# A transformer layer's feed-forward part: weight sums made once by adding DMA transfers, weights loaded in pieces of 512 columns, and the first two output projections run one after the other

## The chip, the cores and the metric

The kernel runs on one core of a Trainium2 chip. The metric is the device time in microseconds (us) of one launch. Five engines work side by side, each on its own list of instructions: PE (TensorE, matrix products; its weight loads are listed apart as PEld), DVE (VectorE), ACT (ScalarE), POOL (GpSimd) and SP (SyncE, which here only issues DMA transfers). They wait for each other through semaphores.

## The reference

For 2048 tokens of width 1024 in float32:

```
h    = rmsnorm(x);  q, k, v of two attention groups = h @ w_in
mix  = concat(differential attention, stick-breaking attention)
x1   = x + mix @ w_out                                # 1024 x 1024
h2   = rmsnorm(x1) * g_ffn
x2   = x1 + (silu(h2 @ w_gate) * (h2 @ w_up)) @ w_down  # width 2816
out  = rmsnorm(x2) * g_final
```

## The kernel before

The program has three stages: projections (0 to 595 us, the function `phase_project`, with a barrier of all engines at its end), attention (595 to about 1485 us), and the output projection with the feed-forward part (the rest, `ffn_programs`). The third stage is the one that is rebuilt.

**Precision.** PE multiplies float32 values as three products: each operand is split into a high part, which ACT writes (`split_hi`, tile `whi` for weights), and a low part, which DVE writes as operand minus high part (`split_lo`, tile `wlo`, line 1665). Only hi*hi, hi*lo and lo*hi are computed. A piece of weights of 128 x 512 is a *unit*. There are seven pairs of `whi` and `wlo` (RING = 7), so a unit can be split as soon as PE has multiplied the one seven before it.

**Blocks and phases.** Tokens go in 4 blocks b of 512. For each block:

- `project(b)`: x1 of block b, 16 units of 12 matmuls each (lines 2108 and 2118). The mixed heads are first turned by PE (`mix_turns`, line 2132, 32 transposes a block) out of the tile `natural`; ACT and DVE split the result (`thi`, `tlo`, lines 1698 and 1929).
- a norm of x1 (`square`, `variance`, POOL's `power`, `scale_in`), 32 transposes of the result on PE (`h2_turns`, line 2154; for block 0 line 2142), copies back (`act_plain`, `dve_plain`), and the seven *operands* of the next phase, split into hi and lo (`prepare_hi`, `prepare_lo`). Four of the operands (s1 to s4) are sums of quarters of h2, made by POOL (`low_sums`, `high_sums`, lines 1611 to 1622).
- `gate_up(b)`: 22 *tiles* of 128 columns of gate and of up. A tile is one Strassen-Winograd step: 7 products instead of 8, each a unit of 12 matmuls of 256 columns (line 2207), so 84 matmuls a tile. The weight operand of a product is a quarter of the tile's weights or a sum of quarters. DVE adds the products up (7 additions of 128 x 256, line 1972: `second`, `third`, `fourth`, `up`, `gate`), ACT copies one (`first`) and computes silu.
- `down(b, half)`: two halves of 22 units each, 12 matmuls of 512 columns a unit. `act` is split in three `stage` slots (`shi`, `slo`).

PE's order before is: project(0), then for each b gate_up(b), down(b, 0), project(b+1) if b < 3, down(b, 1).

**What POOL does in gate_up.** For each of the 88 tiles it makes the weight sums in SBUF out of the two raw weight tiles (`weight_sums`, lines 1581, 1586, 1593 and 1599: four subtractions of 128 x 512) and then the product of silu(gate) and up (line 1606):

```
pool.tensor_tensor(u[:, 0:HALF], u[:, 0:HALF], g[:, 0:HALF], ALU.subtract)   # L1581
pool.tensor_tensor(t2[:], u[:, HALF:D_MODEL], u[:, 0:HALF], ALU.subtract)    # L1586
pool.tensor_tensor(t3[:], t2[:], g[:, 0:HALF], ALU.subtract)                 # L1593
pool.tensor_tensor(t4[:], g[:, HALF:D_MODEL], t2[:], ALU.subtract)           # L1599
pool.tensor_tensor(here, gated[:], up[:], ALU.mult)                          # L1606
```

**Transfers.** SP issues all weight loads in order, as rows of 1024 columns (128 x 1024, 512 KB): two a tile in gate_up, one for two units elsewhere, into 4 raw buffers. POOL issues no transfer. In `phase_project` POOL computes the rotary tables and then stands at the barrier.

## Time and profile before

| | |
|---|---|
| median of 3 runs | 3219.13 us (3218.02 to 3221.1) |
| the profiled execution, its own time | 3216.74 us |
| its span in the trace | 3214.6 us |
| PE busy | 95% of the span |
| DVE, ACT, POOL busy | 69%, 50%, 44% |
| mean granted TensorE clock | 0.986 of full speed |
| moved by DMA | 315.00 MB, mean 98 GB/s |

The median is what a change is measured by. Durations are read from the one profiled execution, whose time is 2.4 us below the median. A matmul's record runs until its result is written, and the next one has begun by then: the distance of the starts is what a matmul costs PE, not the length of its record, and PE reads as busy through short waits.

### The profile page before, as it was taken

What the parts mean: (1) busy time and instruction counts of PE and PEld (TensorE: products, weight loads), DVE (VectorE), ACT (ScalarE), POOL (GpSimd) and SP (SyncE); (2) the same over time, 40 slices, a digit from 0 to 9 for tenths busy, and PEclk for the clock granted to TensorE, in tenths of its full rate; (3) what the DMA queues carried; (4) which work ended last, traced back from release to release, by engine and by line L of the source; (5) the groups of instructions that cost most, each with busy time, mean ns of one, the idle gap of its engine ahead of it and who ended that gap; (6) DMA issues with size and microseconds to landing.
All of it is one profiled execution on the core that took longest, in us unless ns stands there. A gap on an engine that the chain in (4) does not pass through costs nothing.

```text
span 3214.6 us, 52829 instructions
## 1 busy us (share of the span) xinstructions
PE 3048.6 (95%) x19328; PEld 2695.7 (84%) x19328; DVE 2227.4 (69%) x2807; ACT 1602.5 (50%) x2724; POOL 1410.1 (44%) x1128
## 2 busy tenths in 40 slices
PE   7999999899999999998799999899999999999998
PEld 6887788777778999997799888899878998789987
DVE  6224410477776777784899748998479995589964
ACT  5122211477778778874444445444354444444443
POOL 1800000245457777772576204765036670167710
PEclk9999999999999999998899999999999999999999
DMA  5443344522444224112122422233322324223232
GB/s 199 118 122 101 98 132 108 118 44 58 96 106 106 60 60 106 46 39 72 59 93 91 151 97 80 88 121 124 118 73 96 125 91 151 86 85 122 94 98 86
DMA packets 136971, 315.00 MB, mean 98 GB/s; under 512 B 11744, under 2 KB 49376, under 8 KB 136672
## 3 DMA queue, kind: packets, MB, share of 16 engines
q1 hardware_dynamic: 136512, 312.14, 32.4%
q8 instruction: 107, 1.75, 0.2%
q14 instruction: 64, 0.52, 0.1%
q10 hardware_dynamic: 288, 0.59, 0.1%
HBM read 253.96 MB, written 58.72 MB: 97 GB/s over the span
## 4 chain that ended last, share of the span: by engine, by line
PE 23%; DVE 14%; issue 6%; POOL 6%; DMA 1%; DVEq 0%; ACT 0%; POOLq 0%; SPq 0%; ACTq 0%
PE f_ps L2108 18%; DVE f_wlo L1665 9%; PE f_ps L2207 5%; POOL f_act L1606 2%; POOL f_t L1599 2%; DVE f_gate L1972 1%; DMA f_wraw<-in_w_stream 1%; DVE f_up L1972 1%; DVE f_third L1972 1%; DVE f_fourth L1972 1%; POOL f_t L1586 1%; POOL f_wraw L1581 1%; DVE f_slo L1962 0%; POOL f_sum_s L1622 0%; DVE f_second L1972 0%
## 5 line engine op out<-in xcount | busy, mean ns | idle before, releaser
L1665 DVE TENSOR_TENSOR f_wlo<-f_wraw,f_whi 128x512 fp32r<-128x512 f32 x592 | 631.0, 1077 | 114.9 <-ACT f_whi L1656 104.2
L2207 PE MATMUL f_ps<-f_hi_s,f_whi 128*128 128x256 f32 x1408 | 408.4, 290 | 63.5 <-DVE f_up L1972 58.9
L2207 PE MATMUL f_ps<-f_lo_s,f_whi 128*128 128x256 f32 x1408 | 400.6, 285 | 0.0
L2207 PE MATMUL f_ps<-f_hi_s,f_wlo 128*128 128x256 f32 x1408 | 400.1, 284 | 0.0
L1270 POOL TENSOR_TENSOR h_work<-h_work,h_more 128x1024 f32<-128x1024 f32 (+3 forms) x192 | 302.6, 1589 | 110.1 <-DVE h_more L1182 97.2
L2207 PEld LDWEIGHTS f_ps<-f_hi_s,f_whi 128*128 128x128 f32 x1408 | 271.5, 193 | 79.2 <-DVE f_up L1972 68.4
L2207 PE MATMUL f_ps<-f_hi_a,f_whi 128*128 128x256 f32 x1056 | 304.5, 288 | 22.3 <-DVE f_second L1972 13.2
L1665 DVE TENSOR_TENSOR f_wlo<-f_t,f_whi 128x512 fp32r<-128x512 f32 x264 | 304.2, 1152 | 11.5 <-ACT f_whi L1747 11.5
L2207 PE MATMUL f_ps<-f_hi_a,f_wlo 128*128 128x256 f32 x1056 | 301.9, 286 | 0.0
L2207 PE MATMUL f_ps<-f_lo_a,f_whi 128*128 128x256 f32 x1056 | 301.8, 286 | 0.0
L2108 PE MATMUL f_ps<-f_whi,f_shi 128*128 128x512 f32 x696 | 275.3, 396 | 7.7 <-DVE f_slo L1962 7.7
L2108 PE MATMUL f_ps<-f_whi,f_slo 128*128 128x512 f32 x696 | 273.6, 393 | 0.0
L2108 PE MATMUL f_ps<-f_wlo,f_shi 128*128 128x512 f32 x696 | 273.4, 393 | 0.0
L2207 PEld LDWEIGHTS f_ps<-f_hi_s,f_wlo 128*128 128x128 f32 x1408 | 271.8, 193 | 0.0
L1747 ACT ACTIVATE f_whi<-f_wraw 128x512 fp32r<-128x512 f32 x352 | 219.9, 625 | 103.9 <-PE f_ps L2207 93.1
L2207 PEld LDWEIGHTS f_ps<-f_lo_s,f_whi 128*128 128x128 f32 x1408 | 271.7, 193 | 0.0
L1747 ACT ACTIVATE f_whi<-f_t 128x512 fp32r<-128x512 f32 x264 | 166.4, 630 | 197.2 <-PE f_ps L2207 163.2
L1962 DVE TENSOR_TENSOR f_slo<-f_act,f_shi 128x512 fp32r<-128x512 f32 x176 | 133.7, 761 | 186.5 <-ACT f_shi L1737 185.7
L1066 DVE TENSOR_REDUCE h_negmax<-h_z 128x1 f32<-128x1024 f32 (+7 forms) x192 | 166.6, 906 | 138.2 <-PE h_z L672 136.5
L946 PE MATMUL h_o<-h_v,h_attn_t 128*128 128x64 f32 x2176 | 260.3, 273 | 0.0
L946 PEld LDWEIGHTS h_o<-h_v,h_attn_t 128*128 128x128 f32 x2176 | 256.2, 194 | 0.0
L669 PE MATMUL h_z<-h_k,h_qmain 128*128 128x512 f32 (+3 forms) x576 | 222.2, 394 | 21.0 <-ACT h_more L965 6.5
(212 smaller groups left out, 7788.5 us busy)
## 6 DMA issues: line engine op xcount, KB each, us to landing
f_wraw<-in_w_stream SPq DMA_DIRECT2D x296, 512.0 KB, 3.7
qk_scratch<-p_ohi SPq DMA_DIRECT2D x64, 256.0 KB, 2.6
qk_scratch<-p_olo SPq DMA_DIRECT2D x64, 256.0 KB, 3.3
h_k<-qk_scratch SPq DMA_DIRECT2D x32, 512.0 KB, 8.3
h_qmain<-qk_scratch SPq DMA_DIRECT2D x64, 256.0 KB, 12.7
h_qmain<-qk_scratch SPq DMA_DIRECT2D x32, 448.0 KB, 10.8
p_wraw<-in_w_qk SPq DMA_DIRECT2D x16, 512.0 KB, 4.8
v_scratch<-p_vout SPq DMA_DIRECT2D x32, 256.0 KB, 2.0
```

Source lines behind the costliest of these rows:

```text
L669: pe.matmul(out, query(m, 0, seg["tile"]), keys, start=True, stop=False)
L946: mm = pe.matmul(o_bank[use % 2][:, at * HEAD_DIM:(at + 1) * HEAD_DIM], attn_t[e % 2][:, n * P:(n + 1) * P], v_sb[s][:, seg["key_tile"] + ...
L1066: done = dve.tensor_reduce(neg_max[R["set"]][:, col:col + 1], z[t["z"]][:, cols_of(seg)], AX.X, ALU.max, negate=True)
L1270: done = pool.tensor_tensor(part, part, buffer[:, a + 1:b + 1], ALU.mult)
L1599: pool.tensor_tensor(t4[:], g[:, HALF:D_MODEL], t2[:], ALU.subtract).then_inc(S["t_made"], 1)
L1606: pool.tensor_tensor(here, gated[:], up[:], ALU.mult).then_inc(S["act_made"], 1)
L1665: dve.tensor_tensor(w_lo[ring][:], source, w_hi[ring][:].bitcast(F32), ALU.subtract).then_inc(S["lo_split"], 1)
L1747: act.activation(w_hi[ring][:], gate_source(e, i), ACT.Copy).then_inc(S["hi_split"], 1)
L1962: dve.tensor_tensor(stage_lo[v % STAGES][:], act_full[:, v % FT, :], stage_hi[v % STAGES][:].bitcast(F32), ALU.subtract).then_inc(S["stage ...
L1972: add = lambda to, one, other: dve.tensor_tensor(to, one, other, ALU.add).then_inc(S["added"], 1)
L2108: mm = pe.matmul(bank[outs + t][:], a[:, tok], w[u % RING][:], start=(start and n == 0), stop=(stop and n == 2))
L2207: mm = pe.matmul(outs[i], w[ring][:, col], a[name][:, c, :], start=(c == 0 and m == 0), stop=(c == 3 and m == 2))
```

## The change

1. **Weight sums.** At the end of POOL's program in `phase_project` 176 transfers from DRAM to DRAM, of 128 x 512 (256 KB) each, make the four weight sums of all 22 tiles once, in a new DRAM tensor `sums_dram`: 88 plain copies and 88 transfers that add to what is there (`accum_op`). They go in six rounds (44 copies, 44 additions, 22 copies, 22 additions, 22 copies, 22 additions); POOL waits for the whole of a round before the next, but not for the last, and enters the barrier after that. `weight_sums` and its waits are gone from `gate_up`. The signs of the operands and of two of the additions change to suit.
2. **Pieces.** SP loads each unit's weights by itself, 128 x 512 (256 KB), into 7 raw buffers, one for each ring slot: 7 loads a tile in gate_up instead of 2 of double size, and one a unit elsewhere. A load waits until the low part of the unit seven before is split. All units of the stage run through the ring alike; the special orders at the opening of a gate phase are gone.
3. **Product.** The product of silu(gate) and up is DVE's (`product`), in the next tile, after its first addition.
4. **Order.** PE's order is project(0), project(1), then gate_up and down, with project(2) between the halves of down(1) and project(3) between those of down(2). Block 0's norm, transposes and operands are made during project(1), whose turned inputs have a place of their own.
5. `g_final` no longer stays in SBUF but is loaded anew at the second tile of gate_up(1), (2) and (3).

```diff
+            def weights(part, f):
+
+
+                gate = KC + 2 * f
+                return D["w_stream"][gate + part % 2, :, part // 2 * GROUP:(part // 2 + 1) * GROUP]
+
+            for f in range(FT):
+                pool.dma_start(sums_dram[0, f], weights(0, f)).then_inc(sums_stored[0], 16)
+                pool.dma_start(sums_dram[2, f], weights(1, f)).then_inc(sums_stored[2], 16)
+            pool.wait_ge(sums_stored[0], 16 * FT)
+            pool.wait_ge(sums_stored[2], 16 * FT)
+            for f in range(FT):
+                pool.dma_start(sums_dram[0, f], weights(1, f), accum_op=ALU.add).then_inc(sums_stored[0], 16)
+                pool.dma_start(sums_dram[2, f], weights(3, f), accum_op=ALU.add).then_inc(sums_stored[2], 16)
+            pool.wait_ge(sums_stored[0], 2 * 16 * FT)
+            for f in range(FT):
+                pool.dma_start(sums_dram[1, f], sums_dram[0, f]).then_inc(sums_stored[1], 16)
+            pool.wait_ge(sums_stored[1], 16 * FT)
+            for f in range(FT):
+                pool.dma_start(sums_dram[1, f], weights(3, f), accum_op=ALU.add).then_inc(sums_stored[1], 16)
+            pool.wait_ge(sums_stored[1], 2 * 16 * FT)
+            for f in range(FT):
+                pool.dma_start(sums_dram[3, f], sums_dram[1, f]).then_inc(sums_stored[3], 16)
+            pool.wait_ge(sums_stored[3], 16 * FT)
+            for f in range(FT):
+                pool.dma_start(sums_dram[3, f], weights(2, f), accum_op=ALU.add).then_inc(sums_stored[3], 16)
...
+            sp.dma_start(x_sum[1][:], x_blocks[1]).then_inc(S["x_loaded"], 16)
...
+            def load(u, item):
+                sp.wait_ge(S["lo_split"], u - RING + 1)
+                load_plain(sp, F, u, w_stream, item)
+
+            def load_tile(b, f):
+                gate, first_unit = OUT_ITEMS + 2 * f, gate_unit(b) + PRODUCTS * f
+                sources = (w_stream[gate, :, 0:HALF], sums_dram[1, f], sums_dram[0, f], sums_dram[2, f],
+                           w_stream[gate, :, HALF:D_MODEL], sums_dram[3, f], w_stream[gate + 1, :, HALF:D_MODEL])
+                for i, source in enumerate(sources):
+                    u = first_unit + i
+                    sp.wait_ge(S["lo_split"], u - RING + 1)
+                    sp.dma_start(w_raw[u % RING][:], source).then_inc(w_loaded[u % RING], 16)
+
+            sp.wait_ge(S["mix_turned"], ready)
+            sp.dma_start(natural[:], mix_blocks[1]).then_inc(S["mix_loaded"], 16)
+            for u in range(RING, OUT_UNITS):
+                load(u, u // 2)
+            for u in range(OUT_UNITS):
+                load(out_unit(1) + u, u // 2)
+            for sem_of, count in sums_stored:
+                sp.wait_ge(sem_of, count)
...
-                    load_gate(b, f)
+                    load_tile(b, f)
+                    if b and f == 1:
+                        sp.wait_ge(S["side_lo"], PRODUCTS * (b + 1))
+                        sp.dma_start(g_final[:], g_final_dram).then_inc(S["consts"], 16)
...
-            def weight_sums(b, pair, e, opening=False, parts=(1, 2, 3, 4)):
...
-                    pool.tensor_tensor(u[:, 0:HALF], u[:, 0:HALF], g[:, 0:HALF], ALU.subtract).then_inc(S["t_made"], 1)
...
-                    pool.tensor_tensor(t2[:], u[:, HALF:D_MODEL], u[:, 0:HALF], ALU.subtract).then_inc(S["t_made"], 1)
...
-                    pool.tensor_tensor(t3[:], t2[:], g[:, 0:HALF], ALU.subtract).then_inc(S["t_made"], 1)
...
-                    pool.tensor_tensor(t4[:], g[:, HALF:D_MODEL], t2[:], ALU.subtract).then_inc(S["t_made"], 1)
-
-            def product(b, pair, e):
-                tile = tile_of(b, pair, e)
-                pool.wait_ge(S["silued"], tile + 1)
-                pool.wait_ge(S["added"], tile * 7 + 7)
-                here = act_full[:, ds(pair * 2 + e, 1), :].rearrange("p o n -> p (o n)")
-                pool.tensor_tensor(here, gated[:], up[:], ALU.mult).then_inc(S["act_made"], 1)
...
-            power_tiles(0)
+            power(0, 0)
+            low_sums(0)
             high_sums(0)
-            for b in range(BLOCKS):
-                weight_sums(b, 0, 0, True, (4,))
...
-                with pool.Fori(1, pairs - 1) as pair:
-                    weight_sums(b, pair, 1)
-                    product(b, pair - 1, 1)
-                    weight_sums(b, pair + 1, 0)
-                    product(b, pair, 0)
...
+                power(0, b + 1)
+                low_sums(b + 1)
+                high_sums(b + 1)
+            power(1, last - 1)
...
-                    if k + RING < FT or (half == 0):
+                    if u + RING < TOTAL:
                         plain_hi(act, u + RING)
...
             def project(b):
                 for k in range(OUT_UNITS):
-                    if b or k + RING < OUT_UNITS:
-                        plain_hi(act, out_unit(b) + k + RING)
-                    if b == 0:
-                        for i in OPENING_STEPS.get(OUT_UNITS - k, ()):
-                            gate_hi(0, 0, 0, i)
+                    plain_hi(act, out_unit(b) + k + RING)
                     if b == 0 and k == 4:
                         mix_hi(0, range(ready, KC))
-                    if k in (10, 12):
+                    if b == 0 and k in range(10, 14):
+                        mix_hi(1, (k - 10,))
+                    if b == 0 and k >= 14:
+                        mix_hi(1, (2 * k - 24, 2 * k - 23))
+                    if b != 1 and k in (10, 12):
                         square(0, b, 0, (k - 10, k - 9))
+                    if b == 1:
+                        if k in (1, 2):
+                            square(0, 0, 1, (2 * k - 2, 2 * k - 1))
+                        if k in (5, 7):
+                            act_plain(0, (0, 2) if k == 5 else (4, 6))
+                        if k in range(8, 15):
+                            prepare_hi(0, PREPARED[k - 8])
...
+            act.wait_ge(S["consts"], 16)
             project(0)
-            square(0, 0, 1, range(TPB))
-            first_plain()
-            prepare_hi(0, "a11")
-            prepare_hi(0, "a12")
-            act_plain(0, range(4))
-            for name in PREPARED[2:]:
-                prepare_hi(0, name)
+            project(1)
             for b in range(BLOCKS):
                 gate_up(b)
                 down(b, 0)
-                if b < last:
+                if has_out(b):
                     project(b + 1)
                 down(b, 1)
```

How this moves instructions, at three places. The first is DVE in one tile of `gate_up(0)`. Names: `wlo` is the low part of a weight unit, `wraw` raw weights and `t` a weight sum that POOL made (both sources of a split). Before:

```order
L1665 TENSOR_TENSOR f_wlo_4516<-f_wraw_4502,f_whi_4509 128x512
L1972 TENSOR_TENSOR f_second<-f_ps,f_first 128x256
L1665 TENSOR_TENSOR f_wlo_4517<-f_t_4563,f_whi_4510 128x512
L1972 TENSOR_TENSOR f_third<-f_ps,f_second 128x256
L1665 TENSOR_TENSOR f_wlo_4518<-f_wraw_4503,f_whi_4511 128x512
L1972 TENSOR_TENSOR f_fourth<-f_ps,f_second 128x256
L1972 TENSOR_TENSOR f_up<-f_ps,f_fourth 128x256
L1665 TENSOR_TENSOR f_wlo_4519<-f_t_4562,f_whi_4512 128x512
L1972 TENSOR_TENSOR f_gate<-f_ps,f_first 128x256
L1665 TENSOR_TENSOR f_wlo_4520<-f_wraw_4502,f_whi_4513 128x512
L1972 TENSOR_TENSOR f_gate<-f_ps,f_fourth 128x256
L1665 TENSOR_TENSOR f_wlo_4514<-f_t_4554,f_whi_4507 128x512
```

After:

```order
L1604 TENSOR_TENSOR f_wlo_4703<-f_wraw_4689,f_whi_4696 128x512
L1884 TENSOR_TENSOR f_second<-f_ps,f_first 128x256
L1878 TENSOR_TENSOR f_act<-f_gated,f_up 128x512
L1604 TENSOR_TENSOR f_wlo_4704<-f_wraw_4690,f_whi_4697 128x512
L1884 TENSOR_TENSOR f_third<-f_ps,f_second 128x256
L1604 TENSOR_TENSOR f_wlo_4705<-f_wraw_4691,f_whi_4698 128x512
L1884 TENSOR_TENSOR f_fourth<-f_ps,f_second 128x256
L1884 TENSOR_TENSOR f_up<-f_ps,f_fourth 128x256
L1604 TENSOR_TENSOR f_wlo_4699<-f_wraw_4685,f_whi_4692 128x512
L1884 TENSOR_TENSOR f_gate<-f_ps,f_first 128x256
L1604 TENSOR_TENSOR f_wlo_4700<-f_wraw_4686,f_whi_4693 128x512
L1884 TENSOR_TENSOR f_gate<-f_ps,f_fourth 128x256
```

Splits and additions stand as before, seven of each a tile (the rest of the tile goes on in this manner); all splits now read `wraw`, and one instruction is new, `f_act`, the product. On POOL the same stretch held five instructions a tile and now holds none.

The second place is SP, the loads of one tile in gate_up (`sums_scratch` is the DRAM tensor of the sums). Before, two tiles:

```order
L1522 DMA f_wraw_4500<-in_w_stream 128x1024
L1522 DMA f_wraw_4501<-in_w_stream 128x1024
L1522 DMA f_wraw_4502<-in_w_stream 128x1024
L1522 DMA f_wraw_4503<-in_w_stream 128x1024
L1522 DMA f_wraw_4500<-in_w_stream 128x1024
```

After, one tile:

```order
L1511 DMA f_wraw_4689<-in_w_stream 128x512
L1511 DMA f_wraw_4690<-sums_scratch 128x512
L1511 DMA f_wraw_4691<-sums_scratch 128x512
L1511 DMA f_wraw_4685<-sums_scratch 128x512
L1511 DMA f_wraw_4686<-in_w_stream 128x512
L1511 DMA f_wraw_4687<-sums_scratch 128x512
L1511 DMA f_wraw_4688<-in_w_stream 128x512
```

Four of the seven pieces come from the sums, three from the weights as given.

The third place is PE after the last matmuls of project(0). Before (line 2118 the last unit of project(0), 2142 the transposes of block 0's h2, 2207 the first product of gate_up(0)):

```order
L2118 MATMUL f_ps<-f_whi_4508,f_thi 128x512
L2118 MATMUL f_ps<-f_whi_4508,f_tlo 128x512
L2118 MATMUL f_ps<-f_wlo_4515,f_thi 128x512
L2142 MATMUL f_ps<-ident_sb,f_natural 128x128 x32
L2207 MATMUL f_ps<-f_hi_a_4531,f_whi_4509 128x256
L2207 MATMUL f_ps<-f_hi_a_4531,f_wlo_4516 128x256
L2207 MATMUL f_ps<-f_lo_a_4538,f_whi_4509 128x256
```

After (line 2020 units of the projections, 2044 the transposes of `mix_turns` for block 1 in the midst of project(0), before its units 14 and 15):

```order
L2020 MATMUL f_ps<-f_whi_4698,f_thi_4714 128x512
L2020 MATMUL f_ps<-f_whi_4698,f_tlo_4716 128x512
L2020 MATMUL f_ps<-f_wlo_4705,f_thi_4714 128x512
L2044 MATMUL f_ps<-ident_sb,f_natural 128x128 x16
L2020 MATMUL f_ps<-f_whi_4692,f_thi_4714 128x512
L2020 MATMUL f_ps<-f_whi_4692,f_tlo_4716 128x512
```

In the changed program the transposes of h2 (line 2053) stand behind units 4 and 6 of project(1), and the first gate product behind unit 15.

## Rows read from the trace of the kernel before

**Rows 1.** The page, part 1: busy time, share of the span, instructions.

```profile
PE 3048.6 (95%) x19328; PEld 2695.7 (84%) x19328; DVE 2227.4 (69%) x2807; ACT 1602.5 (50%) x2724; POOL 1410.1 (44%) x1128
```

**Rows 2.** Windows, all engines: us, busy (instructions) per engine, clock, DMA share, GB/s.

```profile
150.00:595.00 445.00, 443.79 (x1879) 352.44 (x1877) 119.76 (x166) 88.44 (x137) 3.73 (x3) 1.00 0.39 108
1488.00:1541.00 53.00, 47.23 (x196) 37.91 (x196) 23.65 (x37) 16.81 (x35) 8.75 (x7) 0.94 0.30 101
1541.00:1568.00 27.00, 13.57 (x80) 12.53 (x80) 19.80 (x20) 13.67 (x25) 11.30 (x7) 0.75 0.00 1
...
2100.00:2200.00 100.00, 92.97 (x758) 90.53 (x758) 99.69 (x127) 45.03 (x82) 68.68 (x45) 1.00 0.33 116
```

**Rows 3.** Waits, 2000 to 2235 us: who for whom: us, times, longest.

```profile
PEld f_ps L2207 <- DVE f_up L1972: 19.3, 19, 2.4
PE f_ps L2207 <- DVE f_up L1972: 16.8, 20, 2.2
```

**Rows 4.** Groups of instructions: busy us, mean ns, idle before.

```profile
L1665 DVE TENSOR_TENSOR f_wlo<-f_wraw,f_whi 128x512 fp32r<-128x512 f32 x592 | 631.0, 1077 | 114.9 <-ACT f_whi L1656 104.2 <-ACT f_whi L1747 10.4
...
L1606 POOL TENSOR_TENSOR f_act<-f_gated,f_up 128x512 f32 (+1 forms) x88 | 152.4, 1732 | 56.7 <-DVE f_up L1972 56.7
```

**Rows 5.** Timeline of DVE, 2101 to 2113 us: start, us.

```profile
2101.38 0.68 DVE L1665 TENSOR_TENSOR f_wlo<-f_t,f_whi 128x512 fp32r<-128x512 f32 x1
2101.98 0.42 DVE L1972 TENSOR_TENSOR f_gate<-f_ps,f_first 128x256 f32<-128x256 f32 x1
...
2104.95 3.15 DVE L1665 TENSOR_TENSOR f_wlo<-f_wraw,f_whi 128x512 fp32r<-128x512 f32 x2
```

**Rows 6.** Timeline of PE, 2100 to 2124 us.

```profile
2101.51 0.38 PE L2207 MATMUL f_ps<-f_hi_s,f_whi 128*128 128x256 f32 x1 [0.83 <-DVE f_up L1972]
...
2111.49 0.28 PE L2207 MATMUL f_ps<-f_lo_a,f_whi 128*128 128x256 f32 x1
2112.37 0.38 PE L2207 MATMUL f_ps<-f_hi_s,f_whi 128*128 128x256 f32 x1 [0.60 <-DVE f_up L1972]
```

**Rows 7.** The chain that ended last, in order of time: start, us.

```profile
1807.84 22.07 PE f_ps L2108 x96
...
1985.04 5.69 PE f_ps L2207 x48
...
2223.34 11.70 PE f_ps L2207 x96
...
2412.10 5.76 PE f_ps L2207 x48
...
2648.28 11.70 PE f_ps L2207 x96
...
2830.67 5.75 PE f_ps L2108 x24
...
3073.40 11.70 PE f_ps L2207 x96
```

**Rows 8.** Timeline of PE, 1528 to 1600 us.

```profile
1540.07 0.40 PE L2118 MATMUL f_ps<-f_wlo,f_thi 128*128 128x512 f32 x1
1541.25 3.88 PE L2142 MATMUL f_ps<-ident_sb,f_natural 128*128 128x128 f32 x32 [0.78 <-DVE f_xin L1862]
1551.60 0.55 PE L2207 MATMUL f_ps<-f_hi_a,f_whi 128*128 128x256 f32 x1 [6.46 <-DVE f_natural L1937]
```

**Rows 9.** Timeline of POOL, 150 to 600 us.

```profile
152.86 1.04 POOL L287 TENSOR_SCALAR p_cos<-p_cos 128x1024 f32<-128x1024 f32 x1
595.52 0.11 POOL L1290 MEMSET h_exponent<- 128x16 f32 x1 [441.62 <-POOLq L80]
```

**Rows 10.** DMA, whole execution: transfer, count, KB each, us from issue to landing.

```profile
v_scratch<-p_vout SPq DMA_DIRECT2D x32, 256.0 KB, 2.0
```

**Rows 11.** DMA, 510 to 540 us: GB/s in 40 slices.

```profile
GB/s 0 0 0 0 30 320 0 0 0 0 0 0 322 27 0 0 0 0 0 229 120 0 22 0 0 0 131 229 123 335 330 295 293 290 178 205 161 229 246 232
```

**Rows 12.** Timeline of SP, 596 to 600 us: small loads issued back to back.

```profile
596.38 0.42 SPq L829 DMA_DIRECT2D h_drop<-in_drop  x1
```

436 lines of the change are left out of this document (164 added, 272 removed).

## The prediction

> **What bounds the kernel now.** I read the page first: PE is busy for 95% of the span [rows 1], so time can only come from places where PE waits or computes late. Then the windows of the stage that is rebuilt: in a gate phase, 2100 to 2200 us, DVE is busy for 99.7 of 100 us and PE for 93 [rows 2]; DVE, not PE, sets the pace there. The waits say the same: once a tile, PE and its weight load wait for DVE's addition `up`, some 17 to 19 us in 235 [rows 3]. Then why DVE is full: a split of 128 x 512 takes 1077 ns in the mean over 592 [rows 4], but the timeline has the same instruction twice over, 0.60 us from start to start at 2101.38, and 1.57 us each for a pair at 2104.95 [rows 5]. POOL runs five instructions a tile in the same loop, 1732 ns in the mean for the product, and is busy for 69 of those 100 us [rows 2, 4]. So I take it that DVE and POOL hold each other up where both read two operands from SBUF, and that DVE would need far less alone.
>
> How fast could PE go? A tile starts, after a wait, at 2101.51; its matmuls run to a last start at 2111.49; then comes a wait of 0.60 us, and the next tile's at 2112.37 [rows 6]. So a tile is 10.86 us now and 9.98 + 0.12, less the 0.1 that the first matmul after a wait takes longer: 10.0 us if nothing waits. A phase of 22 tiles would be 220 us.
>
> The phases are longer than that. From the chain, start and end of each: gate_up(1) 1985.04 to 2235.04, 250.0; gate_up(2) 2412.10 to 2659.98, 247.9; gate_up(3) 2836.42 (the end of the row at 2830.67) to 3085.10, 248.7 [rows 7]. Together 746.6, of which 660 is PE's floor. Before gate_up(0), PE ends project(0) at 1540.47 and ends gate_up(0) at 1807.84, where the row of `down` begins: 267.4 us [rows 7, 8]. In there PE waits for the norm and for the operands (3.9 us of transposes, 6.5 us of waiting before the first product), and between 1541 and 1568 its granted clock is 0.75 in the mean, between the levels 2.4 and 1.2 GHz, after it had stood idle [rows 2, 8].
>
> **The change part by part.**
>
> *Gate phases 1 to 3.* With sums and product gone from POOL, POOL has nothing in the loop. DVE's tile is then 7 splits at 0.60, 7 additions at no more than their 0.42 and the product, a split's shape, at 0.60 [rows 5]: 4.2 + 2.9 + 0.6 = 7.7 us of 10.0. The wait for `up` should go, since that addition comes some 1 us after its product and PE has two more products, 2.9 us, before it needs it; the new product stands ahead of it in DVE's list by two steps, and delays it by no more than 0.6. ACT has 7 splits, a copy and a silu a tile, as before, at 45% busy [rows 2]. So PE sets the pace: 660 us, plus what the opening of a phase costs. There DVE has four additions for x2 ahead of the tile and ACT four squares; I allow 2 us a phase, between nothing and the 6.5 us that PE waited before the worst opening now [rows 8]. 746.6 - 666 = **80.6 us gained**.
>
> *The two projections in a row.* Project(1)'s 16 units (22.07 us for 96 matmuls, so 2.76 a unit, 44 us [rows 7]) and its transposes cost the same in either place. What counts is the 267.4 us from the end of project(0) to the end of gate_up(0). After the change they hold, beside project(1): 220 for the gate phase, 3.9 of h2 transposes, and waits that I work out from the order of the steps. Project(1) begins when ACT and DVE have split the last unit and the last two turned chunks, behind project(0)'s last unit: four or five instructions of 0.6 to 0.7 one after another, 3 us. The scaled rows come about when unit 4 ends, 0.5. Its second half waits for copies that are queued behind the split of unit 7, 3 us. The first gate tile waits for the last operand, s4, whose sum POOL makes late, 2 us, and its loads 2 us. Sum 234.4, **33.0 us gained**. Bounds: all waits hidden gives 43.5; a wait of 6.5 us, as before the first product now, at each of the four places would give 17.5.
>
> *Loads in pieces.* A gate tile needs 7 pieces of 256 KB in 10.0 us, 183 GB/s, where the window shows 116 now [rows 2]. SP issues a transfer about every 0.45 us (record of 0.42 [rows 12]), 3.2 us for seven. The 256 KB pieces of attention's first loads move at 290 to 335 GB/s when several are under way [rows 11]. A load is issued when the unit seven before it is split and is needed about 8 us later (seven units are 10.0 us, less the split's two instructions and their waits); such a piece lands in 2.0 us when alone [rows 10]. I cost it at nothing; the cover is that slack, and it is spent if a transfer takes over 1.43 us of the queue's time. The four output stores in the middle of phases 1 to 3 (2 MB, some 7 us at 300 GB/s) use nearly all of it, and I leave up to 2 us each for the range.
>
> The Trainium skill, "DMA: Bandwidth & Descriptors", section "Rules for kernel authors", asks for at least 1 MiB a DMA, and its section "Anatomy of one DMA" fits 2.0 us + bytes/436e3 to one; this speaks against 256 KB pieces. By that, one after another, a tile would need 7 x 2.6 = 18 us of loads. The trace has 335 GB/s with pieces of that size, so they overlap, and I go by the trace.
>
> *The sums in DRAM.* POOL is through with its tables at 153.9 us and then stands for 441.6 us, until the barrier ends at 595.5 [rows 9]. Into this go 154 transfers that it waits for (88 copies and 66 additions), in five rounds; the last 22 additions run on into attention. No row has a transfer by POOL, nor one that adds. Lower bound: the rate of [rows 11], 0.8 us for 256 KB, over the 61% of the DMA engines' time that is free (share 0.39 [rows 2]): 1.3 us each, 200 us. Upper bound: each by itself, issue to landing of the nearest row, 2.0 us [rows 10], and half as long again for an addition's second read: 88 x 2.0 + 66 x 3.0 = 374 us. Both fit; I take about 300 us, and nothing on the path. What it disturbs: SP's loads and stores in the projections, where PE is busy 443.8 of 445 us [rows 2] and raw weights are loaded a unit or more ahead. I take **5 us lost**, from 0 to 20.
>
> *The rest.* The reload of `g_final` lies under gate tiles. In `down` nothing changes but what stood between its halves; its product of the last tile is on DVE, two steps later, with three stages of cover.
>
> Sum: 80.6 + 33.0 - 5 = 108.6 less than the profiled execution's 3216.7: 3108. The median of the runs is 2.4 above that execution: **3110.5 us**, 3.4% less.
>
> **The rivals.**
>
> *A. The chain of sums outlasts the projections (the other side).* All engines wait at the barrier for POOL, so every microsecond past 441.6 is lost. That begins when a transfer costs 441.6/154 = 2.87 us in the mean, and eats the whole gain at (441.6 + 108.6)/154 = 3.6 us. For it: no row shows such a transfer, additions in DRAM read twice, and POOL may need long to issue one. Against it: 2.0 us for the nearest row. At 4.5 us the time would be 3110 + 251 = 3361. In the Trainium skill, "SBUF — State Buffer", section "Who interferes with whom", GpSimd's writing of descriptors can be held up by some DVE instructions; no run here shows that, and by it the issue would lengthen. Overrun but still faster 0.10 (at 3.3 us a transfer 3110 + 67 = 3177), slower than before 0.08.
>
> *B. Loads become the gate phases' bound.* PE would wait for `whi`, ACT for DMA. If a piece took 1.55 us of the queue, a tile would be 10.8 us, as now: 0.8 x 88 = 70 us given back, 3181. For it: seven small loads instead of two large, and the output stores. Against: [rows 11]. 0.10. One at a time, 2.0 us each, a tile would be 14 us: +352, 3463. 0.02.
>
> *C. DVE stays the bound.* If contention with POOL is not what makes splits long, DVE keeps 7 at 1.08 and gains a product: 7.6 + 2.9 + 1.1 = 11.6 us a tile, slower by 0.7 x 88 = 62, less the 33 of the order: 3253. Against it: splits of 0.60 in the same loop, at times when POOL rests. 0.03.
>
> **How the numbers follow.** My forecast has 0.67, with a range of its own of 3090 (no wait left: 86.6 + 43.5 gained) to 3154 (17.5 instead of 33.0 at the first opening, 6.5 us instead of 2 at each of the other three, 20 us of disturbance instead of 5). Above it lie the mild cases of A and B, up to some 3185, with 0.20; beyond, the slower cases with 0.13. The 8-in-10 range is 3088 to 3185. A measurement of this kernel tells 0.2%, 6 us. Faster 0.86, same 0.01, slower 0.13.
>
> **What the changed kernel's profile would show.** Splits of 128 x 512 near 0.68 us in gate phases, DVE at some 75% there and POOL at nothing; gate phases of 222 us; PE without a wait for `up`. PE nearly without a gap from 1540 to the first gate product, and no half-rate stretch there. POOL's last waited-for transfer before 595, PE still full until then. Wrong it would be if attention's first instruction stood later than 595, if ACT in gate phases waited for DMA, or if splits were still over 1 us.

## The result and the profile after

| | before | after |
|---|---|---|
| median of 4 runs | 3218.86 us | 3131.07 us (3128.68 to 3132.69) |
| ratio | | 0.9726, 95% interval 0.9709 to 0.9742 |
| span of the profiled execution | 3214.6 us | 3128.7 us |

87.8 us less, 2.7%; the forecast was 108.6. Below, the page, part 1 (against [rows 1]), and the windows of a gate phase and of the projections (against [rows 2]). A window's line gives its start and end, its length, the busy time and number of instructions of PE, PEld, DVE, ACT and POOL, and then the granted clock, the DMA share and GB/s.

```profile
PE 3015.6 (96%) x19328; PEld 2680.6 (86%) x19328; DVE 1968.4 (63%) x2890; ACT 1610.9 (51%) x2716; POOL 845.3 (27%) x863
```

```profile
1650.00:1850.00 200.00, 200.00 (x1682) 200.00 (x1682) 159.19 (x303) 104.60 (x181) 0.00 (x0) 1.00 0.63 185
150.00:300.00 150.00, 150.00 (x629) 117.95 (x629) 49.12 (x67) 32.79 (x46) 59.48 (x87) 1.00 1.01 255
300.00:450.00 150.00, 145.08 (x585) 110.99 (x584) 65.45 (x92) 32.82 (x53) 63.39 (x95) 0.98 1.04 252
450.00:475.00 25.00, 10.76 (x48) 8.59 (x46) 0.00 (x0) 0.00 (x0) 0.00 (x0) 0.76 1.02 224
```

POOL has nothing to do in this stretch of a gate phase, DVE is busy for 80% where it was 100%, and PE for all of 200 us. In the projections the DMA engines are full from 150 to 475 us, and PE falls to 10.76 of 25 us at the end, with a clock of 0.76 (before, PE was busy for all of 25 us there and the DMA share was 0.20). The splits and the product of a gate phase, against [rows 4], and the chain's rows of the four gate phases, against [rows 7]:

```profile
L1604 DVE TENSOR_TENSOR f_wlo<-f_wraw,f_whi 128x512 fp32r<-128x512 f32 x141 | 97.5, 691 | 40.1 <-ACT f_whi L1597 39.3
...
L1878 DVE TENSOR_TENSOR f_act<-f_gated,f_up 128x512 f32 (+1 forms) x21 | 14.3, 681 | 0.0
```

```profile
1636.50 219.99 PE f_ps L2119 x1848
...
1985.57 219.99 PE f_ps L2119 x1848
...
2382.08 219.99 PE f_ps L2119 x1848
...
2779.15 220.00 PE f_ps L2119 x1848
```

1848 matmuls in 220.0 us, 10.0 a tile, in every phase, with no wait at an opening. The rest of the gain has to be read against losses. POOL's timeline from the tables to the barrier, against [rows 9] (the 44 transfers of round 1 or 2 alternate between two lines of the kernel, so only the first of each round is shown; a row has its start, its length, and in brackets how long the engine stood idle before it and what ended that):

```profile
155.14 0.82 POOL L297 DMA_DIRECT2D sums_scratch<-in_w_stream  x1 [0.32 <-POOL p_cos L288]
...
215.45 0.89 POOL L302 DMA_DIRECT2D sums_scratch<-in_w_stream  x1 [37.25 <-DMA sums_scratch<-in_w_stream]
```

```profile
316.93 10.59 POOL L306 DMA_DIRECT2D sums_scratch<-sums_scratch  x22 [11.73 <-DMA sums_scratch<-in_w_stream]
345.37 18.50 POOL L309 DMA_DIRECT2D sums_scratch<-in_w_stream  x22 [17.85 <-DMA sums_scratch<-sums_scratch]
391.74 10.61 POOL L312 DMA_DIRECT2D sums_scratch<-sums_scratch  x22 [27.87 <-DMA sums_scratch<-in_w_stream]
418.98 18.49 POOL L315 DMA_DIRECT2D sums_scratch<-in_w_stream  x22 [16.63 <-DMA sums_scratch<-sums_scratch]
```

```profile
621.12 0.11 POOL L1318 MEMSET h_exponent<- 128x16 f32 x1 [183.64 <-POOLq L81]
```

Round 1 (44 copies) takes 60.3 us, round 2 (44 additions) 101.5, then 28.4, 46.4 and 27.2 for 22 each: a copy costs 1.24 to 1.37 us, an addition 2.11 to 2.31. In all 154 transfers take 263.8 us, fewer than the 300 of the forecast, and POOL is done at 437.5; its wait of 183.64 us shows that the barrier waits for others. The barrier ends at 621.12, 25.6 us later than before. In the six kernels here that have this same first stage (this one, e2, e4, e5, e7 and e9) it ends between 615.5 and 622.8, so one trace places this loss only to some microseconds. Who waited, 410 to 480 us, and SP's list there (from about 434 us PE makes the values, in the value stage, and SP stores them):

```profile
ACT p_vout L377 <- DMA v_scratch<-p_vout: 37.4, 2, 35.9
...
PE p_ps L574 <- ACT p_vout L377: 15.4, 1, 15.4
...
ACT p_vhi L371 <- DMA p_vraw<-in_w_v: 6.4, 1, 6.4
...
PE p_rot L538 <- ACT p_rawqk L347: 4.9, 1, 4.9
```

```profile
449.52 4.37 SPq L172 DMA_DIRECT2D p_vraw<-in_w_v  x4
453.94 30.76 SPq L177 DMA_DIRECT2D v_scratch<-p_vout  x7
```

PE stands still twice: for 4.9 us until 420.13, because ACT's copy of a result is queued behind the split of raw value weights that land late, and for 15.4 us until 476.20, because all four output banks are full. ACT can't empty them until the first value store has landed; SP issued it at 453.94 (before: 438.51), and it landed at 475.5. The granted clock is 0.50, that is 1.2 GHz, from 465 to 480 us and from 420 to 425, behind these waits. SP's transfers landed late as a whole (median us, last number; before, the two kinds of `qk_scratch` stores took 2.6 and 3.3 and the value weights 5.3; the value stores keep the median of 2.0 of [rows 10], but their longest is 21.5, where it was 14.3):

```profile
sums_scratch<-in_w_stream POOLq DMA_DIRECT2D x132, 256.0 KB, 21.2
qk_scratch<-p_ohi SPq DMA_DIRECT2D x64, 256.0 KB, 7.4
qk_scratch<-p_olo SPq DMA_DIRECT2D x64, 256.0 KB, 9.5
...
p_vraw<-in_w_v SPq DMA_DIRECT2D x16, 256.0 KB, 14.7
```

The first output projection has a wait of its own:

```profile
1530.91 0.36 SPq L1514 DMA_DIRECT2D f_natural<-mix_scratch  x1
...
1531.31 20.11 SPq L1445 DMA_DIRECT2D f_wraw<-in_w_stream  x14
...
1539.81 0.63 ACT L1597 ACTIVATE f_whi<-f_wraw 128x512 fp32r<-128x512 f32 x1 [21.25 <-DMA f_wraw<-in_w_stream]
...
1545.09 0.76 PE L2020 MATMUL f_ps<-f_whi,f_thi 128*128 128x512 f32 x1 [11.68 <-DVE f_tlo L1846]
```

SP stands for the landing of attention's last output, issues the 2 MB of mix block 1, and then the weights, which share the queue with it. ACT has no weights for 21.25 us, the copy of the last turned chunk is queued behind that split, and PE waits 11.68 us, where it waited 5.1 before.

The account in us, from the traces: gate phases 1 to 3, 746.6 - 660.0 = +86.6. From the end of project(0) to the end of gate_up(0): before 267.4, and project(1) took 48.1 in its old place (177.2 from 1807.84 to 1985.04 [rows 7], less 129.1 for the two halves of the same down without it, after); after 277.4 with project(1) in it: +38.1. Project(0) itself 52.4 before, 62.9 after: -10.5. Projections -25.6, attention -2.5. Sum 86.1, and the spans differ by 85.9.

### The profile page after: what moved, and what is told of

It is laid out like the page before. It is cut to its first block, busy times and chain, and to the rows that moved or that the text cites. A ratio compares the mean times of both kernels' runs of the same rounds, so it can differ in the third digit from the quotient of the medians.

```text
span 3128.7 us, 52437 instructions
## 1 busy us (share of the span) xinstructions
PE 3015.6 (96%) x19328; PEld 2680.6 (86%) x19328; DVE 1968.4 (63%) x2890; ACT 1610.9 (51%) x2716; POOL 845.3 (27%) x863
## 4 chain that ended last, share of the span: by engine, by line
PE 61%; DVE 9%; POOL 6%; ACT 3%; issue 1%; DMA 0%; DVEq 0%; SPq 0%; ACTq 0%; POOLq 0%
PE f_ps L2119 28%; PE f_ps L2020 18%; PE h_o L974 6%; PE h_t L960 3%; PE h_z L697 2%; PE h_z L700 2%; DVE h_negmax L1094 2%; POOL h_more L1258 2%; POOL h_work L1258 2%; DVE h_more L1210 2%; DVE h_more L1126 1%; POOL h_srstd L1303 1%; ACT h_work L993 1%; ACT h_more L993 1%; POOL f_sum_s L1576 1%
## 5 line engine op out<-in xcount | busy, mean ns | idle before, releaser
L1604 DVE TENSOR_TENSOR f_wlo<-f_wraw,f_whi 128x512 fp32r<-128x512 f32 x856 | 598.7, 700 | 284.5 <-ACT f_whi L1597 282.4
L1597 ACT ACTIVATE f_whi<-f_wraw 128x512 fp32r<-128x512 f32 x856 | 535.5, 627 | 458.1 <-PE f_ps L2119 301.0
L2119 PE MATMUL f_ps<-f_hi_s,f_whi 128*128 128x256 f32 x1408 | 397.1, 282 | 0.0
L1554 POOL TENSOR_TENSOR f_rstd<-f_var,f_exponent 128x4 f32<-128x4 f32 x7 | 7.1, 1009 | 1100.8 <-DVE f_var L1824 1100.8
L2119 PE MATMUL f_ps<-f_hi_a,f_whi 128*128 128x256 f32 x1056 | 297.5, 282 | 0.0
L1210 DVE TENSOR_TENSOR_SCAN h_more<-h_z,h_zero 128x1024 f32<-128x1024 f32 (+7 forms) x128 | 232.0, 1813 | 7.4
## 6 DMA issues: line engine op xcount, KB each, us to landing
h_qmain<-qk_scratch SPq DMA_DIRECT2D x32, 448.0 KB, 10.8
```

Source lines behind the costliest of these rows:

```text
L1210: done = dve.tensor_tensor_scan(buffer[:, a:b][:, ::-1], z[cur["z"]][:, cols_of(seg)][:, ::-1], zero[:].to_broadcast([P, seg["tiles"] * P] ...
L1597: act.activation(w_hi[ring][:], w_raw[ring][:], ACT.Copy).then_inc(S["hi_split"], 1)
L1604: dve.tensor_tensor(w_lo[ring][:], w_raw[ring][:], w_hi[ring][:].bitcast(F32), ALU.subtract).then_inc(S["lo_split"], 1)
L2119: mm = pe.matmul(outs[i], w[ring][:, col], a[name][:, c, :], start=(c == 0 and m == 0), stop=(c == 3 and m == 2))
```

## The experiments

Each is an edit of the changed kernel (3131.07, ratio 0.9726). "Barrier" is the end of the projections, "stretch" the time from project(0)'s first product to gate_up(0)'s. Ratios are to the kernel before. The medians are of four or five executions; barrier and stretch are from the one that was profiled, which for e9 and e11 was the slowest of the five (3119.58 and 3099.08 us).

| run | median us | ratio, 95% interval | barrier | stretch |
|---|---|---|---|---|
| changed kernel | 3131.07 | 0.9726 (0.9709 to 0.9742) | 621.1 | 120.2 |
| e1 no sums | 3104.43 | 0.9644 (0.9630 to 0.9659) | 595.8 | 122.2 |
| e2 mix behind weights | 3127.00 | 0.9712 (0.9699 to 0.9726) | 615.5 | 124.1 |
| e3 copies before tables | 3115.14 | 0.9675 (0.9662 to 0.9688) | 607.5 | 119.2 |
| e4 work on POOL | 3189.42 | 0.9905 (0.9889 to 0.9920) | 618.4 | 122.1 |
| e5 four weights before store | 3124.34 | 0.9705 (0.9692 to 0.9719) | 619.6 | 116.3 |
| e6 value stores first | 3117.21 | 0.9677 (0.9663 to 0.9690) | 606.1 | 122.6 |
| e7 old order | 3138.20 | 0.9748 (0.9733 to 0.9763) | 618.5 | |
| e8 copies spread | 3117.14 | 0.9681 (0.9667 to 0.9694) | 608.8 | 118.7 |
| e9 five weights before store | 3113.44 | 0.9672 (0.9657 to 0.9687) | 622.8 | 107.1 |
| e10 e9 and e6 | 3101.06 | 0.9632 (0.9618 to 0.9646) | 608.5 | 108.3 |
| e11 e10 and e8 | 3094.65 | 0.9609 (0.9593 to 0.9625) | 599.7 | 109.8 |
| e12 copies for additions | 3100.95 | 0.9631 (0.9618 to 0.9644) | 595.8 | 119.0 |

### Where the projections lost 25.6 us: e1, e3, e6, e8, e12

e1 takes the sums away; the gate phases load other weights of the same size in their place, so its output is not the layer's:

```diff
-            for f in range(FT):
-                pool.dma_start(sums_dram[0, f], weights(0, f)).then_inc(sums_stored[0], 16)
...
-                sources = (w_stream[gate, :, 0:HALF], sums_dram[1, f], sums_dram[0, f], sums_dram[2, f],
+                sources = (w_stream[gate, :, 0:HALF], w_stream[gate + 1, :, 0:HALF], w_stream[gate, :, 0:HALF], w_stream[gate + 1, :, 0:HALF],
```

> The changed kernel without the 176 transfers that make the sums; the gate loads of sums take a plain piece of the gate weights in their place, as many and as large (so the sums are wrong by content, the work of the engines is the same). Theory: the transfers fill the DMA engines until 475 us and delay SP's stores and loads; all of the 25.6 us that the projections lost is theirs, in two waits of PE (4.92 at 420.13 and 15.44 at 476.20) and the half clock behind them. Then the barrier ends near 595.5 as before the change, the time falls by 25 to 28 us to 3103 to 3106, PE has no wait over 1 us between 150 and 540, and stores of qk_scratch land in 2.5 to 3.3 us again. Rival: the projections lost their time to something else in the new build (placement, the list of SP), then less than 5 us comes back. The 11 us longer first output projection must stay in either case.

3104.43 us, the barrier at 595.75, PE without a wait from 150 to 595 us, the `qk_scratch` stores at 2.6 and 3.2 us again: the whole loss is the transfers'. The stretch stays at 122.2, so project(0)'s loss is another thing.

e3 issues the first 44 copies ahead of POOL's tables:

```diff
+            for f in range(FT):
+                pool.dma_start(sums_dram[0, f], weights(0, f)).then_inc(sums_stored[0], 16)
+                pool.dma_start(sums_dram[2, f], weights(1, f)).then_inc(sums_stored[2], 16)
             pool.wait_ge(consts, 48)
```

> The changed kernel with the first 44 copies of the sums issued by POOL ahead of its sine and cosine tables (near 79 us) and not behind them (155); same transfers otherwise. Theory: what costs 25.6 us is not the amount of traffic but that its last rounds meet the change from the key and query stores to the value projection (415 to 475 us). The chain then ends some 40 us earlier (copies land under the tables, near 175; POOL starts round 2 at 177 instead of 215), round 6 is over by about 435, the value stage finds free queues, and 10 to 20 us come back: 3111 to 3121. Rival: the traffic disturbs wherever it lies; then the copies cost PE as much at 80 to 150 as the end gains, and the time stays within 4 us of 3131, or grows if weight loads of the first units come late.

3115.14, inside the range. Its windows:

```profile
80.00:150.00 70.00, 60.41 (x252) 48.41 (x251) 13.49 (x17) 10.20 (x16) 49.75 (x33) 0.93 0.74 221
...
450.00:500.00 50.00, 50.00 (x222) 41.42 (x221) 0.00 (x0) 5.99 (x10) 0.00 (x0) 1.00 0.38 115
```

The value stage is whole again (34.6 of 50 us in the changed kernel), and 9.6 us are lost at 80 to 150, where PE waits 8.3 us for DVE, DVE for ACT, and ACT 25.0 us for a `qk_scratch` store to land: both theories hold by half. The place of a burst decides: the same 44 copies cost nothing from 155 to 215 us in the changed kernel, where PE is busy for all of the window, and 9.6 us at 80.

e6 changes only SP's list, and leaves the sums as they are:

```diff
+            for n in range(12, 2 * KC):
+                load_v(n)
+            for m in range(TPB):
+                store_v(m)
             for b in range(BLOCKS):
                 sp.wait_ge(stored[b], (TILES + 1) * 32)
             load_queries(sp, H["q_last"][0], qk_scratch, 0, LAST_TILE, SEQ, 0, H["late_keys"][0])
```

> The changed kernel with SP's wait for the last key and query stores, and the three loads of attention's first keys and queries behind it, moved behind the first four stores of values; the chain of sums is as in the changed kernel. Theory: PE's 15.4 us at 476.20 are made by the order in SP's list: the first value store is issued only at 453.94, behind the wait for stores that now take 8 us to land and behind 1.3 MB of loads in a full queue. Then that store goes out some 10 us earlier with nothing ahead of it and PE's wait falls to under 5 us; with the half clock behind it 12 to 18 us come back: 3113 to 3119. The wait of 4.9 us at 420 stays. Rival: a store in the full queue takes 15 us or more wherever it stands; then at most 5 us come back.

3117.21, as the theory has it. The first value store goes out at 438.46 instead of 453.94; a value store still takes up to 24.7 us to land, so the rival is right about the store and wrong about the price: PE now waits 2.3 us for it. The wait at the other place stays, at 5.8 us.

```profile
PE p_rot L540 <- ACT p_rawqk L349: 5.8, 1, 5.8
...
PE p_ps L576 <- ACT p_vout L379: 2.3, 1, 2.3
```

e8 spreads the first copies between the tables:

```diff
+            def paced(instruction):
+                chain(instruction)
+                copy_next()
...
-                chain(pool.tensor_copy(cos, cos.bitcast(I32)))
+                paced(pool.tensor_copy(cos, cos.bitcast(I32)))
```

> The changed kernel with the first 44 copies of the sums issued one by one between the 40 instructions of POOL's tables (79 to 177 us), not in a row ahead of them or behind. Theory: the sums cost PE time only where a burst meets a stage that waits for stores or loads. Issued in a row at 79 they cost about 10 us there (PE busy 60.4 of 70 us) and freed the value stage; spread out, one copy each 2.3 us, they should cost 0 to 3 us and free the value stage as well, so that nearly all of 25.6 us comes back: 3105 to 3109, as without any sums (3104.4). Rival: at 80 to 150 us the queues have no room for any transfer of these (16 loads of 512 KB with stores between): then 3112 to 3116 as with copies in a row.

3117.14: missed, just above the rival's range too. Spreading costs nothing, as the theory said, but it does not free the value stage, where PE waits 11.3 us: I had reckoned with the end of the copies and not with that of the chain, which ends only 19 us earlier (last addition issued at 418.8 instead of 437.5; in e3 it was 399.7), and so still runs into the first value stores.

```profile
80.00:150.00 70.00, 70.00 (x305) 56.84 (x304) 12.90 (x16) 10.63 (x16) 60.62 (x54) 1.00 0.75 211
...
450.00:500.00 50.00, 38.71 (x163) 31.50 (x162) 0.00 (x0) 5.98 (x10) 0.00 (x0) 0.90 0.34 103
```

e12 makes the 88 additions plain copies (`accum_op=ALU.add` left out four times), so that its output is another.

> The changed kernel with the 88 adding transfers made plain copies of the same size, in the same order and with the same waits (the additions of the weight sums are left out, so the output is another). Theory: the chain is long because an addition of 256 KB takes 2.1 to 2.3 us of the DMA engines where a copy takes 1.24 to 1.37. With copies alone the 154 transfers that are waited for take 1.3 us each, 200 us in place of 264, the last 22 another 29; the chain ends near 385 us, ahead of the value stage, and the time is that without any sums or up to 4 us more: 3104 to 3109. Rival: POOL's own writing of the transfers (it is held 53 us in the second round) and the wait from round to round set the length; then the chain still runs past 430 us and the time stays over 3120.

3100.95, even under the range; the barrier is at 595.81, and PE has no wait from 150 to 595 us. POOL's first two rounds begin at:

```profile
154.78 0.81 POOL L297 DMA_DIRECT2D sums_scratch<-in_w_stream  x1 [0.31 <-POOL p_cos L288]
...
216.93 0.52 POOL L302 DMA_DIRECT2D sums_scratch<-in_w_stream  x1 [39.16 <-DMA sums_scratch<-in_w_stream]
```

Rounds 1 and 2 now take 62 us each, the wait of 52.69 us within round 2 is gone, and the last issue is over at 381 instead of 437.5. So as many transfers of the same size cost PE nothing when they end before the value stage; what carried the chain into it is that an addition takes 2.1 to 2.3 us and a copy 1.2 to 1.4. e3 says the same from the other side: with every addition in it, but the last issued at 399.7, the value stage is whole.

### Project(0): e2, e5, e9

e2 puts four weight loads between SP's wait and the 2 MB of mix block 1.

```diff
-            sp.dma_start(natural[:], mix_blocks[1]).then_inc(S["mix_loaded"], 16)
             for u in range(RING, OUT_UNITS):
+                if u == RING + 4:
+                    sp.dma_start(natural[:], mix_blocks[1]).then_inc(S["mix_loaded"], 16)
```

> The changed kernel with SP's load of mix block 1 (2 MB) issued behind the loads of units 7 to 10 and not ahead of them; nothing else. Theory: in the changed kernel the weights stand in the queue behind that 2 MB (first of them waited for 9.3 us), ACT and DVE stand still for them, and PE waits 11.7 us at 1545 for the last turned chunks, where it waited 5.1 before the change. Then PE's wait falls back to about 5 us, its clock over the projection rises from 0.90, and the time falls by 6 to 11 us to 3120 to 3125. Rival: the wait comes from the order of the steps (chunk 7's copy behind unit 7), and then the time stays within 2 us of 3131.

3127.00, missed: PE waits 12.86 us at the same place, and the stretch is 4 us longer, not shorter. The 4 us by which the median fell did not come from here (in the trace the barrier is 5.7 us earlier and attention 4.4 us shorter, and neither was changed). SP comes to these loads only at 1520.87, when attention's last output has landed, and the split that stands ahead of the last chunk's copy is that of unit 11, whose load is behind the 2 MB here too. e5 and e9 therefore issue the loads before x block 1, and so before that store and the wait for it, e5 units 7 to 10 and e9 unit 11 as well:

```diff
         def sync_ahead(sp):
+            for u in range(RING, RING + 5):
+                load(sp, u, u // 2)
             sp.dma_start(x_sum[1][:], x_blocks[1]).then_inc(S["x_loaded"], 16)
```

> The changed kernel with SP's loads of units 7 to 10 issued ahead of its load of x block 1, and so ahead of the store of attention's last output and of the wait for its landing; the 2 MB of mix block 1 come behind them. The run with those loads merely in front of mix block 1 gave 4 us, and PE still waited 12.9 us there, because SP stood until 1520.87 for the landing of that store and the next weight (unit 11 by count) then shared the queue with 2 MB. Theory: what is late is the weights' issue, which the kernel before had ahead of that wait. Then ACT has units 7 to 10 at once, chunk 7's copy is not queued behind a late split, PE's wait at the end of unit 3 falls from 12.9 to about 5 us (as before the change) or less, and the time is 3118 to 3122. Rival: PE waits for the norm of the last heads (copy of chunk 7 by DVE and ACT) as long in any case; then 3125 to 3127, like the run before.

> As the run with the loads of units 7 to 10 ahead of the store, but with unit 11 as well, five loads. There PE still waited 8.29 us at 1534.59: in ACT's order the split of unit 11 stands in front of the copy of chunk 7, and its load came behind the 2 MB of mix block 1 and landed at 1532.4. Theory: with unit 11 there in time, the copy of chunk 7 waits for the norm of the last heads alone, and PE's wait falls to between 0 and 5 us; another 3 to 8 us come back: 3115 to 3121. Rival: the next split in line (unit 12) or the norm takes its place; then the wait stays at 8 and the time at 3124.

e5 3124.34, between the range of the theory and that of the rival; ACT and PE there, with the load of unit 11 landing for 1532.42:

```profile
1532.42 0.63 ACT L1600 ACTIVATE f_whi<-f_wraw 128x512 fp32r<-128x512 f32 x1 [11.33 <-DMA f_wraw<-in_w_stream]
...
1534.59 0.76 PE L2023 MATMUL f_ps<-f_whi,f_thi 128*128 128x512 f32 x1 [8.29 <-DVE f_tlo L1849]
```

e9 3113.44, a larger gain than expected: that wait of PE is gone, and the stretch is 107.1 us, 13 less than in the changed kernel and 9 less than in e5. The load of unit 11 decides it.

### DVE and POOL: e4

```diff
+                with pool.Fori(2, FT) as f:
+                    for i in range(EXTRA):
+                        pool.wait_ge(S["multiplied"], gate_unit(b) + f * PRODUCTS + i + 1)
+                        pool.wait_ge(S["extra"], extras(b) + (f - 2) * EXTRA + i + 1)
+                        pool.tensor_tensor(F["extra"][:], F["extra"][:], F["extra"][:], ALU.subtract).then_inc(S["extra"], 1)
```

> The changed kernel with five subtractions of 128 x 512 on POOL in each gate tile from the third on (a scratch tile minus itself, paced by PE's products; 100 a phase), whose result nobody uses; the output is the same. Theory: a split on DVE is long (1.08 us in the mean before the change, 0.70 after) because POOL works on two operands from SBUF at the same time. Then splits go back to about 1.0 to 1.1 us in the mean, DVE needs 7 x 1.08 + 2.9 + about 1.1 = 11.6 us a tile and becomes the bound, and 80 tiles get 1.0 to 1.6 us longer: 3211 to 3260. Rival: splits became shorter because they read pieces of 512 columns from tiles of their own, or because of the order on DVE; then they stay at 0.70 and the time within 5 us of 3131.

3189.42, 58 us slower. The same window as above:

```profile
1650.00:1850.00 200.00, 197.15 (x1618) 193.30 (x1616) 184.73 (x288) 100.77 (x174) 129.13 (x95) 1.00 0.60 176
```

```profile
L1597 POOL TENSOR_TENSOR f_extra<-f_extra 128x512 f32<-128x512 f32 x95 | 129.1, 1359 | 86.1 <-PE f_ps L2130 80.3
L1615 DVE TENSOR_TENSOR f_wlo<-f_wraw,f_whi 128x512 fp32r<-128x512 f32 x134 | 124.1, 926 | 14.6 <-ACT f_whi L1608 14.6
...
L1889 DVE TENSOR_TENSOR f_act<-f_gated,f_up 128x512 f32 (+1 forms) x19 | 22.6, 1191 | 0.0
```

With POOL working in SBUF, splits go from 691 to 926 ns and the product from 681 to 1191; 7 x 0.926 + 7 x 0.41 + 1.19 = 10.5 us a tile, and the pieces of 24 matmuls on the chain come every 10.41 us. That is gate_up(0); gate_up(1) to (3) take 237 to 239 us, 10.8 a tile, 713.8 together, so e4 gives back 54 of the 86.6 us that these phases gained. So it is shown that POOL's work lengthens DVE's, and the size was overstated: I took the 1.08 us of before. That figure is a mean over the whole stage; in steady tiles of gate_up(0) before, 1650 to 1800 us, the splits were longer still:

```profile
L1665 DVE TENSOR_TENSOR f_wlo<-f_wraw,f_whi 128x512 fp32r<-128x512 f32 x55 | 73.6, 1356 | 0.4 <-ACT f_whi L1747 0.4
L1665 DVE TENSOR_TENSOR f_wlo<-f_t,f_whi 128x512 fp32r<-128x512 f32 x42 | 50.4, 1200 | 0.0
```

Their mean is 1278 ns, 587 more than after the change, and e4 brings back 235 of these, 40%, with POOL busy for 65% of the time where it was 69%. What the other 60% are is open. POOL's five instructions of before took 1.39 to 1.73 us each and most read two tiles, these take 1.36 and read one; the raw tiles and DVE's order are others too, and no run separates these, nor POOL's reads from its writes. The Trainium skill, "SBUF — State Buffer", section "Who interferes with whom", says that a DVE instruction with two SBUF inputs contends with a GpSimd instruction that reads SBUF; this run is in keeping with it, and the additions, which take one input from PSUM, stay at 0.41 us.

### The order: e7

e7 puts project(1) back between the halves of down(0), with block 0's norm between project(0) and gate_up(0):

```diff
-    return 1 <= b < BLOCKS - 1
+    return b < BLOCKS - 1
...
             project(0)
-            project(1)
+            pe.wait_ge(S["x1_half"], 2 * TPB)
+            pe.wait_ge(S["scaled"], TPB)
+            h2_turns(0, range(KC))
```

> The changed kernel with the second output projection back between the halves of the first down projection, where the kernel before had it, with the norm of block 0 then standing between projection 0 and gate phase 0 (done by the block, not tile by tile as in the kernel before, which makes it a few us longer); sums, pieces and DVE's product as in the changed kernel. Theory: project(1) covered the norm and the operands. From the end of project(0) to the end of gate_up(0), with project(1) wherever it is, the changed kernel has 277.4 - 48.1 = 229.3 us and would now have 220 + 25 to 32 for additions, squares, scaling, 3.9 of transposes, copies, sums and the first operands: 245 to 252. Against it stand some 7 to 11 us of project(0), which no longer has 2 MB of mix block 1 in its queue. Net 3139 to 3150. Rival: the order gave nothing and the whole gain of that region came from the faster gate phase; then 3120 to 3131.

3138.20, just under the range. On its chain, project(0) ends at 1567.72 and gate_up(0) at 1816.93:

```profile
1537.90 29.82 PE f_ps L1991 x120
...
1605.29 211.64 PE f_ps L2073 x1776
1816.93 13.24 PE f_ps L1991 x58
```

That is 249.2 us, in the range of 245 to 252, where the changed kernel has 229.3: against e7 the order is worth 19.9 us, of which project(0) gives 9.1 back (53.8 us without mix block 1 in its queue, 62.9 with it); the medians are 7.1 us apart. But e7 makes block 0's norm by the block, where the kernel before made it tile by tile: from project(0)'s end to the first gate product e7 takes 19.9 us (1567.72 to 1587.57), the kernel before 11.1 (1540.47 to 1551.60). So up to 8.8 of the 19.9 us are the price of that norm and not of the order, and how the 38.1 us divide between the order and tiles that no longer wait for DVE is not settled.

### Together: e10, e11

> The changed kernel with two moves in SP's list: five weight loads ahead of attention's last store and the first four value stores ahead of attention's first loads; the sums as in the changed kernel. If the two causes are independent, the gains add: 13.9 us of the value stores and 7 to 15 of the weights: 3102 to 3111. What stays is the wait of 5 to 6 us at 420 for late raw value weights with the half clock behind it.

> As the run before it, with the first 44 copies of the sums spread between the tables as well, so that the chain ends some 19 us earlier. Theory: each of the three places is then free of waits: no wait at 420 (as with the spread copies), none over 2.5 us in the value stage, barrier at 596 to 599 us where it was 595.5 before the change, and project(0) without the wait for chunk 7: 3131.1 - 24 - 7 to 15 = 3092 to 3100, 3.7 to 4.0% under the kernel before. Rival: the value stores land late as long as any of the chain runs (last adds issued to 419), and 3 to 8 us of it stay: 3100 to 3107.

e10 3101.06, 1 us under its range; e11 3094.65, ratio 0.9609, the fastest of all and 3.9% under the kernel before, inside its range. In e11 the barrier is at 599.67. PE still waits 2.4 us at the first place, where none was expected, and the value stage is whole:

```profile
400.00:450.00 50.00, 47.57 (x194) 36.99 (x193) 15.58 (x23) 10.41 (x18) 12.32 (x15) 0.97 1.04 238
450.00:500.00 50.00, 50.00 (x223) 41.41 (x222) 0.00 (x0) 5.38 (x9) 0.00 (x0) 1.00 0.37 100
```

## Why the prediction was right in sign and 21 us too low

Forecast 3110.5 us, measured 3131.1, within the range. The nearness is in part luck: the gate phases and the region behind project(0) gave 11.1 us more than forecast, and this hid a third of the 33.6 us that the sums, project(0) and attention lost beyond it. By its steps:

**Gate phases 1 to 3: right.** 86.6 us for 80.6. Splits 0.69 us, DVE 80% busy, no wait for `up`, PE's 10.0 us a tile: each as forecast. The 2 us a phase that I allowed for openings were not lost. Rival C did not happen: the splits did not stay at 1.08 us. The reason named, POOL's work beside DVE's, is shown by e4 for 40% of what the splits lost in length and for 54 of the 86.6 us; the rest is argued.

**Loads in pieces at nothing: right.** 185 GB/s in the window, pieces land in 2.7 to 2.8 us, and PE never waits for one in a gate phase. The rule of the Trainium skill ("DMA: Bandwidth & Descriptors", "Rules for kernel authors"), at least 1 MiB a transfer, is given there for the highest bandwidth. It spoke against the pieces, but no gate phase asks for the highest: 256 KB pieces, several under way, brought the 185 GB/s that were needed. The fit that the prediction quotes beside it stands there for transfers that GpSimd issues; these are SP's. The row that the step leaned on, [rows 11], was read too simply: from 529.91 us one load of 1 MB and four of 448 KB are under way there beside eight of 256 KB, so its 290 to 335 GB/s are not a rate of 256 KB pieces alone.

**The region behind project(0): right in sum.** 38.1 for 33.0. Its waits were 2.9 us (forecast 3), 1.5 (0.5), 2.9 (3) and none (4). One sign failed: behind the first of them the matmuls from 1582.9 to 1585.5 us stand 0.43 us apart and not 0.23, at a granted clock of 0.75 from 1580 to 1585, where I had written that there would be no half-rate stretch.

**Project(0): a step that was not in the forecast**, 10.5 us lost. I wrote that project(0) and project(1) cost the same in either place and started the count at project(0)'s end. What was missed is a transfer that moved along: the load of mix block 1 moved ahead of the weights in SP's list, and the two early weight loads of the kernel before were no longer in front of the wait for attention's store. Without mix block 1 there (e7) project(0) takes 53.8 us, near the 52.4 of before; with it, but with five loads in front of the store (e9), the stretch is 13 us shorter.

**The sums: the length was right, the price was the term that failed.** "5 us lost, from 0 to 20" measured 25.6 (e1), and by the prediction's own sign the step is wrong: attention begins at 621 us and not by 595. Duration and place (263.8 us inside 441.6) were near the forecast. The cover that I named, raw weights loaded ahead, held from 150 to 400 us: PE was full there with the DMA share over 1. It ran out at two places. At 420 us it was raw weights after all, those of the values, which landed late: 4.9 us. The larger part, 15.4 us, was a store with an engine waiting behind it, which the step did not count at all: four output banks hang on it, and it stands behind 3.25 MiB of loads (e6). The window's mean over the projections, 443.8 of 445 us, hid that place. Rival A, the chain outlasting the projections, did not happen, and nor did B, loads as the bound of the gate phases.

## What to carry to other kernels

A background stream of transfers is not priced by whether it fits in idle time, but by the tightest store or load that it meets: here the same stream cost nothing from 150 to 400 us and some 25 behind that. Look for the place where compute waits for a landing, and let the stream end before it, or move that transfer forward in its queue. When work is moved, write out the issuing engine's list before and after, and ask of each load which wait now stands in front of it; here one 256 KB load behind such a wait was worth some 10 us. Work on POOL beside a full DVE has a price on DVE: in e4 five subtractions lengthened DVE's instructions by 2.2 us a tile (7 x 0.235 + 0.51). Measure it in the steady loop, and not from a mean over a stage.
